# Expert layers of a two-layer encoder step: the last item's down weights go through the gate weights' buffers

## The chip, the cores and the metric

The kernel runs on one core of one Trainium2 chip. The metric is the device time of one execution in microseconds (us); the figure quoted for a kernel is the median of its runs. Engines are named as the profile names them: PE is TensorE, DVE is VectorE, ACT is ScalarE, POOL is GpSimd, SP is SyncE, which here only issues DMAs.

## What is computed

The reference is one inference step of a streaming encoder of two layers (`D_MODEL` 1024) for two groups of rows, 512 prompt frames and 32 sample frames, 544 rows in all. Each layer is a normalised mixer (attention), a gated residual, and then a grouped top-2 mixture of 16 experts with a gated residual. Only the mixture matters here:

```python
def _moe(h, w_router, b_router, w_gate, w_up, w_down):
    ...
    a = jax.nn.silu(jnp.einsum('nd,edf->nef', t, w_gate)) * jnp.einsum('nd,edf->nef', t, w_up)
    a = a * gates[:, :, None].astype(a.dtype)
    return jnp.einsum('nef,efd->nd', a, w_down).reshape(B, T, D)
```

`gates` is zero but for two experts of each row. `w_gate` and `w_up` are 1024 x 512 for each expert, `w_down` is 512 x 1024, all float32.

## The kernel before

**Items.** The router stage sorts the 1088 pairs of a row and an expert by expert and cuts them into items of up to 128 rows with one expert each; 18 items in layer 0 and 16 in layer 1 in the profiled execution. The expert stage `moe0` or `moe1` handles one item after another. For an item, the rows are gathered from DRAM and transposed, multiplied by the gate and by the up weights (8 steps of 128 along the 1024 each), silu(gate) times up gives the activations, these are transposed, and multiplied by the down weights (4 steps along the 512, two halves of 512 output columns). The result, scaled by the row's gate, is scattered to DRAM by an indirect DMA from POOL. After the last item, the stage `combine` reads both results of every row back and adds them to `x`.

**Split products.** float32 is multiplied as three products of rounded parts: high x high, high x low, low x high (`split_product`, lines 580 to 584). So each weight slab is split after it has landed: ACT copies it rounded into a second buffer (the high part, `split_high`, line 1899), then DVE and POOL subtract that from the landed slab in place (the low part; DVE's pieces 0, 2 and 3 in `split_low`, line 1905, POOL's piece 1 at line 2373). A slab of 2 MB is 128 x 4096, in four pieces of 128 x 1024, and comes in two DMAs of two pieces each.

**Buffers.** There is one landed slab and one high slab for each of gate, up and down: `m_low` is the three parts of `ring`, `m_high` lies in `hT`, `work` and `arena` (line 1877). So a load can start only when PE is done with the slab's previous user. In the expert stage SP (`moe_sync`, its loads at line 2128) takes them in this order: in `turn(n)` it waits until the gate product of item n is done and loads the gate weights of item n+1, waits for the up product of n and loads up for n+1, waits for the down product of item n-1 and loads down for item n.

**Order of each engine.** PE does gate(n), transposes of the rows of n+1, up(n), down(n-1), transposes of the activations of n (line 2215). The down product is thus one item behind. In the code, `down_before(n)` is the product of item n-1, and counts of the down slab carry the same shift. After the loop each engine has the last item written out. On PE it is gate(last), up(last), down of the item before the last, transposes, down of the last item, which in this code is `down_before(last + 1)`. On ACT it is: activations high (line 2272), the second half of the up split, silu (line 2268), the split of the down weights of the item before the last, `results_before(last)` (two scaled copies out of the banks, line 2280, which first wait for the scatter of the item before them, `s["y"]`), `act_high_before(last + 1)` (line 2272), the split of the last item's down weights, `results_before(last + 1)`. On DVE: the low part of the activations (line 2339), low splits of up and down, `product(last)` (line 2335), `act_low_before(last + 1)` (line 2339), the low split of the last down weights. On POOL: its piece of the down split, `rows_out_before(last)` (line 1994 copies the row numbers, line 1997 is the scatter), its piece of the last down split, `rows_out_before(last + 1)`. SP waits for `s["d"] >= last`, so for the down product of the item before the last, loads the last item's down weights, waits for all scatters (`s["y"]`), and issues the reads for `combine` (lines 2168 and 2172).

The stages are separated by `phase_end`: PE, ACT, DVE and POOL all have to reach it. SP isn't held by it, but its own order is fixed.

Of the kernel before, what the change touches and what calls it, by code (L numbers as in the profile page):

```python
# [18 lines left out]
ACT = mybir.ActivationFunctionType  # L19
# [56 lines left out]
def encoder_step(nc, a, out, rope_dram):  # L76
    ctx = ExitStack()
    with ctx:
# [3 lines left out]
        def sems(prefix, *names):  # L82
            return {n: ctx.enter_context(nc.semaphore(f"{prefix}_{n}")) for n in names}
# [1768 lines left out]
        def out_pool(pool, l):  # L1852
            s, o = NORM, 2 * l + 1
            for j in OUT_POOL:
# [8 lines left out]

        MO = sems("mo", "wg0", "wg1", "wu0", "wu1", "wd0", "wd1", "hi_g", "hi_u", "hi_d", "lo_g", "lo_u", "lo_d",
                  "lop_g", "lop_u", "lop_d", "x", "tx", "xh", "xl", "g", "sg", "u", "a", "at", "ah", "al", "d", "ev", "y", "now_tok", "now_out")
        m_x = arena[:, 0:1024]
        m_xh = arena[:, 1024:2048].rearrange("p (k c) -> p k c", k=KD)
# [6 lines left out]
        SLAB = KD * CB  # L1876
        m_low = {"g": ring[:, 0, :], "u": ring[:, 1, :], "d": ring[:, 2, :]}
        m_high = {"g": hT_flat[:, 0:SLAB], "u": work[:, 0:SLAB], "d": arena[:, 10240:10240 + SLAB]}

        def piece(v, q):  # L1880
            return v[:, SLAB // 4 * q:SLAB // 4 * (q + 1)]
# [9 lines left out]

            return 0 if l == 0 else eng.value_load(n_items[0:1, 4:5], min_val=9, max_val=MAX_ITEMS)

        def split_high(act, c, n, *pieces):

            for q in pieces:
                if q in (0, 2):
                    act.wait_ge(MO[f"w{c}{q // 2}"], 16 * n if c == "d" else 16 * n + 16)
                act.activation(r32(piece(m_high[c], q)), piece(m_low[c], q), ACT.Copy).then_inc(MO[f"hi_{c}"], 1)  # L1899

        def split_low(dve, c, n, *pieces):

            for q in pieces:
                dve.wait_ge(MO[f"hi_{c}"], 4 * n + q + 1)
                dve.tensor_tensor(r32(piece(m_low[c], q)), piece(m_low[c], q), f32(piece(m_high[c], q)),  # L1905
                                  ALU.subtract).then_inc(MO[f"lo_{c}"], 1)


# [211 lines left out]
        def moe_sync(sp, l):  # L2120
            s = MO
            slabs = {"g": (a["w_gate"][l], KD), "u": (a["w_up"][l], KD), "d": (a["w_down"][l], KE)}

            def load(c, e):
                w, k = slabs[c]
                w = w[bass.ds(e, 1), :, :].rearrange("a (p k) c -> p (a k) c", k=k)
                for h in range(2):
                    sp.dma_start(m_low[c][:, SLAB // 2 * h:SLAB // 2 * (h + 1)].rearrange("p (k c) -> p k c", k=k // 2),
                                 w[:, k // 2 * h:k // 2 * (h + 1), :]).then_inc(s[f"w{c}{h}"], 16)


            sp.wait_ge(OUT["mm"], 10 * (l + 1))
            for c in "gud":
                load(c, 0)
            o = NORM_NO[f"norm_ffn{l}"]
            sp.wait_ge(NORM["shifted"], 3 * o + 3)
            sp.wait_ge(NORM["shift_v"], 2 * o + 2)
            sp.dma_start(moe_in[0:SEQ, :].rearrange("(t p) d -> p t d", p=P), h_rows[:, 0:NT, :]).then_inc(RT["h"], 16)
            sp.dma_start(moe_in[SEQ:TOK, :], h_rows[0:DEC, NT, :]).then_inc(RT["h"], 16)
            sp.wait_ge(g["phase"], PH[f"route{l}"])  # L2140
            first, last, end = first_item(sp, l), item_no(sp, "last"), item_no(sp, "end")

            def expert(n):
                i = nc.s_assert_within(n - first, 0, MAX_ITEMS - 1, skip_runtime_bounds_check_because="n is an item of this layer")
                return sp.value_load(item_expert[0:1, bass.ds(i, 1)], min_val=0, max_val=NE - 1)

            def turn(n, down):

                e = expert(n + 1)
                sp.wait_ge(s["g"], n + 1)  # L2150
                load("g", e)
                sp.wait_ge(s["u"], n + 1)
                load("u", e)
                if down:
                    e = expert(n)
                    sp.wait_ge(s["d"], n)
                    load("d", e)

            turn(first, False)
            with sp.Fori(first + 1, last) as n:  # L2160
                turn(n, True)
            e = expert(last)
            sp.wait_ge(s["d"], last)
            load("d", e)
            sp.wait_ge(s["y"], 16 * end)
            for t in range(TILES):
                if t < NT:
                    sp.dma_start(arena[:, 2 * D * t:2 * D * (t + 1)].rearrange("p (c d) -> p c d", c=2),
                                 moe_out.rearrange("(c n) d -> n c d", c=2)[P * t:P * (t + 1), :, :]).then_inc(CO[f"y{t}"], 32)
                else:  # L2170
                    for c in range(2):
                        sp.dma_start(c_y[t][c][0:DEC, :], moe_out[TOK * c + SEQ:TOK * (c + 1), :]).then_inc(CO[f"y{t}"], 16)

        def moe_pe(pe, l):
# [40 lines left out]
                    last_ = nc.tensor.transpose(bank[6][:, P * k:P * k + P], ak[:, k, :], ident[:, :])  # L2215
                last_.then_inc(s["at"], 1)

            def down_before(n):

                pe.wait_ge(s["al"], n)  # L2220
                hi, lo = (r32(v["d"].rearrange("p (k c) -> p k c", k=KE)) for v in (m_high, m_low))
                for k in range(KE):
                    wait_piece("d", n, k)
                    for h in range(2):
                        c = slice(CB * h, CB * h + CB)
                        last_ = split_product(bank[4 + h][:, :], r32(m_ah[:, k, :]), r32(m_al[:, k, :]), hi[:, k, c],
                                              lo[:, k, c], k == 0, k == KE - 1)
                last_.then_inc(s["d"], 1)
# [13 lines left out]
            gate_or_up("u", last)  # L2242
            down_before(last)
            turn_act(last)
            down_before(last + 1)
            phase_end("pe", pe)

        def moe_act(act, l):
# [57 lines left out]
            split("u", last, 2, 3)  # L2306
            silu(last)
            split("d", last, 0, 1, 2, 3)
            results_before(last, last_1)
            act_high_before(last + 1)  # L2310
            split("d", last + 1, 0, 1, 2, 3)
            results_before(last + 1, last)
            phase_end("act", act)

        def moe_dve(dve, l):
# [44 lines left out]
            split("u", last, 2, 3)  # L2360
            split("d", last, 0, 2, 3)
            product(last)
            act_low_before(last + 1)
            split("d", last + 1, 0, 2, 3)
            phase_end("dve", dve)

        def moe_pool(pool, l):
            first, last = first_item(pool, l), item_no(pool, "last")

            def split(c, n):  # L2370
                pool.wait_ge(MO[f"hi_{c}"], 4 * n + 2)
                settle(pool)
                pool.tensor_tensor(r32(piece(m_low[c], 1)), piece(m_low[c], 1), f32(piece(m_high[c], 1)),  # L2373
                                   ALU.subtract).then_inc(MO[f"lop_{c}"], 1)

            def item(n):
# [26 lines left out]
                turn(n, True)  # L2403
            turn(last_1, False)
            split("d", last)
            rows_out_before(last)
            split("d", last + 1)
            rows_out_before(last + 1)
            phase_end("pool", pool)

# [189 lines left out]
```

## Time and profile before

| | us |
|---|---|
| median of 3 runs | 1777.8 |
| lowest and highest of them | 1762.39, 1778.7 |
| the profiled execution, its time | 1779.54 |
| the profiled execution, its span | 1777.8 |
| its mean granted TensorE clock | 0.913 |

The page's times and all rows below come from the profiled execution, and count from the start of its span. The two expert stages end at about 903 us and 1732 us. "Line" is the line of the kernel; buffer numbers are left out of names, so `ring` is any of the three landed slabs and `arena_r` among other things the high part of down, `hT_r` that of gate, `work_r` that of up.

### The profile page before, as it was taken

To read this page: it belongs to the slowest core of one execution; us is meant where nothing else is said; L and a number is where in the kernel's file an instruction comes from. 1 tells how busy PE (TensorE), PEld (TensorE's weight loads), DVE (VectorE), ACT (ScalarE), POOL (GpSimd) and SP (SyncE) were. 2 spreads that over 40 slices of the span, in tenths; PEclk is the share of its full clock that TensorE was granted. 3 is DMA by queue.
4 is the path that set the end of the run, shared out by engine and by line. 5 is a ranking of instruction groups with operands and counts; after the bars stand their busy time and mean duration, and the time that the engine had idled before them with its cause. 6 is when DMAs were issued, how large, how long until landed. Compare 5 with 4: busy or idle time off the path is not lost. (4 is left out here: it accounts for less than half of the span.)

```text
span 1777.8 us, 22790 instructions
## 1 busy us (share of the span) xinstructions
PE 1496.0 (84%) x7971; PEld 1170.2 (66%) x7979; DVE 1027.2 (58%) x1341; ACT 863.7 (49%) x1512; POOL 498.2 (28%) x383
## 2 busy tenths in 40 slices
PE   3399999997947999999916999999889399999970
PEld 0387777764736877777715877777567277887760
DVE  0545532225455899899856433343363568889865
ACT  2233334445124877777614333343341268878751
POOL 1200111110104666566421000000001246666531
PEclk8699999998977999999956999999889599999985
DMA  8245553133044999899661333442421379999944
GB/s 282 74 159 188 177 183 102 67 127 102 1 192 155 380 350 347 341 360 347 264 239 50 97 102 102 130 145 97 155 71 63 140 287 374 368 368 370 351 188 173
DMA packets 148608, 358.62 MB, mean 202 GB/s; under 512 B 18660, under 2 KB 80868, under 8 KB 122420
## 3 DMA queue, kind: packets, MB, share of 16 engines
q1 hardware_dynamic: 136184, 333.25, 52.0%
q0 software_dynamic: 12352, 24.40, 3.7%
q8 instruction: 45, 0.74, 0.2%
q14 instruction: 27, 0.22, 0.0%
HBM read 341.87 MB, written 33.56 MB: 211 GB/s over the span
## 5 line engine op out<-in xcount | busy, mean ns | idle before, releaser
L583 PE MATMUL bank<-ring_r,arena_r 128*128 128x512 f32 x816 | 323.9, 397 | 0.0
L582 PE MATMUL bank<-ring_r,hT_r 128*128 128x384 f32 x640 | 238.7, 373 | 4.3 <-DVE ring_r L637 4.3
L584 PE MATMUL bank<-ring_r,work_r 128*128 128x384 f32 x640 | 216.9, 339 | 0.0
L583 PE MATMUL bank<-ring_r,hT_r 128*128 128x384 f32 x640 | 216.7, 339 | 0.0
L1905 DVE TENSOR_TENSOR ring_r<-ring,arena_r 128x1024 fp32r<-128x1024 f32 x102 | 169.5, 1698 | 40.3 <-ACT arena_r L1899 40.2
L1905 DVE TENSOR_TENSOR ring_r<-ring,work_r 128x1024 fp32r<-128x1024 f32 x102 | 175.0, 1741 | 28.6 <-ACT work_r L1899 28.5
L583 PEld LDWEIGHTS bank<-ring_r,arena_r 128*128 128x128 f32 x816 | 157.4, 193 | 31.3
L1905 DVE TENSOR_TENSOR ring_r<-ring,hT_r 128x1024 fp32r<-128x1024 f32 x102 | 145.9, 1458 | 25.0 <-ACT hT_r L1899 23.9
L1899 ACT ACTIVATE hT_r<-ring 128x1024 fp32r<-128x1024 f32 x136 | 136.2, 1054 | 37.7 <-DMA ring<-in_w_gate 37.7
L582 PEld LDWEIGHTS bank<-ring_r,hT_r 128*128 128x128 f32 x640 | 121.3, 190 | 45.5 <-issue 43.5
L1899 ACT ACTIVATE arena_r<-ring 128x1024 fp32r<-128x1024 f32 x136 | 134.6, 1051 | 27.4 <-DMA ring<-in_w_down 27.2
L1899 ACT ACTIVATE work_r<-ring 128x1024 fp32r<-128x1024 f32 x136 | 136.6, 1059 | 7.1 <-DMA ring<-in_w_up 7.0
L1858 POOL TENSOR_TENSOR arena<-arena,bc 128x1024 f32<-128x1024 f32 (+1 forms) x6 | 14.3, 2386 | 441.2 <-DVE arena L1844 441.2
L582 PE MATMUL bank<-arena_r 128*128 128x512 f32 x272 | 109.5, 402 | 19.6 <-DVE ring_r L1905 19.6
L583 PEld LDWEIGHTS bank<-ring_r,hT_r 128*128 128x128 f32 x640 | 121.7, 190 | 1.2 <-issue 0.7
L584 PEld LDWEIGHTS bank<-ring_r,work_r 128*128 128x128 f32 x640 | 121.0, 189 | 0.0
L2373 POOL TENSOR_TENSOR ring_r<-ring,arena_r 128x1024 fp32r<-128x1024 f32 x34 | 91.7, 2696 | 95.9 <-ACT arena_r L1899 95.9
L582 PE MATMUL bank<-hT_r,arena_r 128*128 128x512 f32 x272 | 114.5, 421 | 3.1 <-ACT arena_r L2262 3.0
L584 PE MATMUL bank<-hT_r,arena_r 128*128 128x512 f32 x272 | 110.8, 407 | 0.0
L582 PE MATMUL bank<-work_r,arena_r 128*128 128x512 f32 x272 | 109.2, 402 | 0.0
L680 ACT ACTIVATE arena<-bank 128x384 f32<-128x384 f32 (+1 forms) x48 | 23.4, 488 | 175.0 <-PE bank L584 175.0
L584 PE MATMUL bank<-arena_r 128*128 128x512 f32 x272 | 107.9, 397 | 0.0
(357 smaller groups left out, 2980.6 us busy)
## 6 DMA issues: line engine op xcount, KB each, us to landing
ring<-in_w_gate SPq DMA_DIRECT2D x68, 1024.0 KB, 6.9
ring<-in_w_up SPq DMA_DIRECT2D x68, 1024.0 KB, 7.3
ring<-in_w_down SPq DMA_DIRECT2D x68, 1024.0 KB, 7.2
bc<-in_w_ada SPq DMA_DIRECT2D x40, 1024.0 KB, 6.8
bc<-in_w_in_even SPq DMA_DIRECT2D x64, 192.0 KB, 3.9
bc<-in_w_in_odd SPq DMA_DIRECT2D x64, 192.0 KB, 3.5
ring<-in_w_ada SPq DMA_DIRECT2D x4, 2048.0 KB, 11.8
arena<-moe_out SPq DMA_DIRECT2D x8, 1024.0 KB
```

Of the source, the lines that this page charges most:

```text
L582: nc.tensor.matmul(acc, rows_hi, w_hi, start=first, stop=False)
L583: nc.tensor.matmul(acc, rows_hi, w_lo, start=False, stop=False)
L584: return nc.tensor.matmul(acc, rows_lo, w_hi, start=False, stop=last)
L680: act.activation(fu_rows[b % 2][0:rows(t), t, :], bank[n % 2][0:rows(t), 0:BW], ACT.Copy).then_inc(FU["ev_a"], 1)
L1858: pool.tensor_tensor(h_rows[0:r, t, :], h_rows[0:r, t, :], scale_shift(f"norm_ffn{l}", t)[1], ALU.add).then_inc(s["shifted"], 1)
L1899: act.activation(r32(piece(m_high[c], q)), piece(m_low[c], q), ACT.Copy).then_inc(MO[f"hi_{c}"], 1)
L1905: dve.tensor_tensor(r32(piece(m_low[c], q)), piece(m_low[c], q), f32(piece(m_high[c], q)), ALU.subtract).then_inc(MO[f"lo_{c}"], 1)
L2373: pool.tensor_tensor(r32(piece(m_low[c], 1)), piece(m_low[c], 1), f32(piece(m_high[c], 1)), ALU.subtract).then_inc(MO[f"lop_{c}"], 1)
```

## The change

For the last item of each layer alone, the down weights are loaded into the gate slab (`ring` part 0) and their high part is written to `hT`, where the gate's high part lay. SP issues that load when the gate product of the last item is done instead of when the down product of the item before the last is done. The load has two semaphores of its own, `wl0` and `wl1`; those of the down slab are raised by SP after its wait for the scatters so that their counts stay right. On ACT the high split moves ahead of `results_before(last)`; on DVE the low split moves ahead of `act_low_before(last + 1)`; on POOL its piece moves ahead of `rows_out_before(last)`. PE takes its operands from the other buffers. The diff, cut to its core:

```diff
+        def slab_of(c, last_down):
+            return "g" if last_down else c
...
-        def split_high(act, c, n, *pieces):
+        def split_high(act, c, n, *pieces, last_down=None):
+            v = slab_of(c, last_down is not None)
             for q in pieces:
                 if q in (0, 2):
-                    act.wait_ge(MO[f"w{c}{q // 2}"], 16 * n if c == "d" else 16 * n + 16)
-                act.activation(r32(piece(m_high[c], q)), piece(m_low[c], q), ACT.Copy).then_inc(MO[f"hi_{c}"], 1)
+                    if last_down is not None:
+                        act.wait_ge(MO[f"wl{q // 2}"], 16 * last_down + 16)
+                    else:
+                        act.wait_ge(MO[f"w{c}{q // 2}"], 16 * n if c == "d" else 16 * n + 16)
+                act.activation(r32(piece(m_high[v], q)), piece(m_low[v], q), ACT.Copy).then_inc(MO[f"hi_{c}"], 1)
...
             e = expert(last)
-            sp.wait_ge(s["d"], last)
-            load("d", e)
+            sp.wait_ge(s["g"], last + 1)
+            load("d", e, last_down=True)
             sp.wait_ge(s["y"], 16 * end)
+            for h in range(2):
+                sp.sem_inc(s[f"wd{h}"], 16)
...
             down_before(last)
             turn_act(last)
-            down_before(last + 1)
+            down_before(last + 1, last_down=True)
             phase_end("pe", pe)
...
             split("d", last, 0, 1, 2, 3)
+            split_high(act, "d", last + 1, 0, 1, 2, 3, last_down=l)
             results_before(last, last_1)
             act_high_before(last + 1)
-            split("d", last + 1, 0, 1, 2, 3)
             results_before(last + 1, last)
...
             split("d", last, 0, 2, 3)
             product(last)
+            split_low(dve, "d", last + 1, 0, 2, 3, last_down=True)
             act_low_before(last + 1)
-            split("d", last + 1, 0, 2, 3)
             phase_end("dve", dve)
...
             split("d", last)
+            split("d", last + 1, last_down=True)
             rows_out_before(last)
-            split("d", last + 1)
             rows_out_before(last + 1)
             phase_end("pool", pool)
```

## Rows read from the trace of the kernel before

**Rows 1.** The page: an engine's busy time, share of the span, instructions.

```profile
PE 1496.0 (84%) x7971; PEld 1170.2 (66%) x7979; DVE 1027.2 (58%) x1341; ACT 863.7 (49%) x1512; POOL 498.2 (28%) x383
```

**Rows 2.** Timeline of PE, end of layer 1: start us, duration us, engine, line.

```profile
1710.20 0.47 PE L582 MATMUL bank<-arena_r 128*128 128x512 f32 x1 [1.27 <-DVE ring_r L1905]
...
1715.76 0.63 PE L2215 MATMUL bank<-ident,arena 128*128 128x128 f32 x4
1723.29 0.79 PE L582 MATMUL bank<-arena_r 128*128 128x512 f32 x1 [6.89 <-DVE ring_r L1905]
```

**Rows 3.** Timeline of ACT, end of layer 1.

```profile
1703.44 0.60 ACT L2268 ACTIVATE arena<-bank 128x512 f32<-128x512 f32 x1 [0.23 <-PE bank L584]
1703.94 3.89 ACT L1899 ACTIVATE arena_r<-ring 128x1024 fp32r<-128x1024 f32 x4
1716.22 1.27 ACT L2280 ACTIVATE arena<-bank,slot_gate 128x512 f32<-128x512 f32 x2 [8.39 <-PE bank L584]
...
1720.92 2.00 ACT L1899 ACTIVATE arena_r<-ring 128x1024 fp32r<-128x1024 f32 x2 [2.94 <-DMA ring<-in_w_down]
1723.82 2.00 ACT L1899 ACTIVATE arena_r<-ring 128x1024 fp32r<-128x1024 f32 x2 [0.90 <-DMA ring<-in_w_down]
1732.04 1.27 ACT L2280 ACTIVATE arena<-bank,slot_gate 128x512 f32<-128x512 f32 x2 [6.22 <-PE bank L584]
```

**Rows 4.** Timeline of DVE, end of layer 1.

```profile
1706.63 5.70 DVE L1905 TENSOR_TENSOR ring_r<-ring,arena_r 128x1024 fp32r<-128x1024 f32 x3
1712.24 0.68 DVE L2335 TENSOR_TENSOR arena<-bank,arena 128x512 f32<-128x512 f32 x1
1718.01 0.69 DVE L2339 TENSOR_TENSOR arena_r<-bank,arena_r 128x512 fp32r<-128x512 f32 x1 [5.09 <-ACT arena_r L2272]
1722.01 1.23 DVE L1905 TENSOR_TENSOR ring_r<-ring,arena_r 128x1024 fp32r<-128x1024 f32 x1 [3.30 <-ACT arena_r L1899]
```

**Rows 5.** Timeline of POOL, end of layer 1.

```profile
1693.10 3.28 POOL L2373 TENSOR_TENSOR ring_r<-ring,hT_r 128x1024 fp32r<-128x1024 f32 x1 [2.36 <-ACT hT_r L1899]
...
1706.12 2.85 POOL L2373 TENSOR_TENSOR ring_r<-ring,arena_r 128x1024 fp32r<-128x1024 f32 x1 [1.64 <-ACT arena_r L1899]
...
1734.52 1.00 POOL L1997 DMA_INDIRECT moe_out<-arena,now_out  x1 [0.86 <-POOL now_out L1994]
```

**Rows 6.** Timeline of SP: its DMA issues, two answers.

```profile
1716.11 0.85 SPq L2128 DMA_DIRECT2D ring<-in_w_down  x2
...
1737.79 2.09 SPq L2168 DMA_DIRECT2D arena<-moe_out  x4
```

**Rows 7.** Windows: stretch, busy PE PEld DVE ACT POOL, PEclk, DMA share, GB/s.

```profile
1704.50:1706.00 1.50, 1.50 (x8) 1.24 (x7) 1.50 (x2) 1.50 (x3) 0.00 (x0) 1.00 0.39 156
...
1723.29:1731.90 8.61, 8.60 (x24) 6.49 (x24) 2.80 (x2) 2.00 (x2) 2.20 (x1) 0.64 0.08 30
```

**Rows 8.** Instructions of one tile: its DMAs' landing, for ring, then for moe_out.

```profile
DMA to landing us min/median/max: 4.8/7.1/17.9
...
DMA to landing us min/median/max: 3.2/7.1/12.7
```

**Rows 9.** Timelines of PE, DVE and ACT, end of layer 0.

```profile
894.49 0.79 PE L582 MATMUL bank<-arena_r 128*128 128x512 f32 x1 [6.94 <-DVE ring_r L1905]
...
889.09 0.69 DVE L2339 TENSOR_TENSOR arena_r<-bank,arena_r 128x512 fp32r<-128x512 f32 x1 [4.98 <-ACT arena_r L2272]
...
902.94 1.26 ACT L2280 ACTIVATE arena<-bank,slot_gate 128x512 f32<-128x512 f32 x2 [4.69 <-PE bank L584]
```

**Rows 10.** Shorter stalls of PE in the item loops, and windows behind them.

```profile
810.29 0.72 PE L2215 MATMUL bank<-ident,arena 128*128 128x128 f32 x4 [1.73 <-DVE arena L2335]
...
1435.47 0.84 PE L2215 MATMUL bank<-ident,arena 128*128 128x128 f32 x4 [3.30 <-DVE arena L2335]
...
811.00:814.80 3.80, 3.80 (x11) 3.01 (x11) 3.80 (x5) 3.30 (x4) 2.89 (x3) 0.55 0.99 374
655.60:659.00 3.40, 3.40 (x15) 2.80 (x16) 3.40 (x5) 3.26 (x4) 2.49 (x3) 1.00 0.99 419
```

More of the change, by code:

```diff
@@ L1859, in out_pool @@
             phase_end("pool", pool)
-        MO = sems("mo", "wg0", "wg1", "wu0", "wu1", "wd0", "wd1", "hi_g", "hi_u", "hi_d", "lo_g", "lo_u", "lo_d",
+        MO = sems("mo", "wg0", "wg1", "wu0", "wu1", "wd0", "wd1", "wl0", "wl1", "hi_g", "hi_u", "hi_d", "lo_g", "lo_u", "lo_d",
                   "lop_g", "lop_u", "lop_d", "x", "tx", "xh", "xl", "g", "sg", "u", "a", "at", "ah", "al", "d", "ev", "y", "now_tok", "now_out")
@@ L1892, in layer_first, with split_low @@
             return 0 if l == 0 else eng.value_load(n_items[0:1, 4:5], min_val=9, max_val=MAX_ITEMS)
-        def split_high(act, c, n, *pieces):
+        def split_high(act, c, n, *pieces, last_down=None):
+            v = slab_of(c, last_down is not None)
             for q in pieces:
                 if q in (0, 2):
-                    act.wait_ge(MO[f"w{c}{q // 2}"], 16 * n if c == "d" else 16 * n + 16)
-                act.activation(r32(piece(m_high[c], q)), piece(m_low[c], q), ACT.Copy).then_inc(MO[f"hi_{c}"], 1)
-        def split_low(dve, c, n, *pieces):
+                    if last_down is not None:
[3 more added lines that the diff above has]
+                act.activation(r32(piece(m_high[v], q)), piece(m_low[v], q), ACT.Copy).then_inc(MO[f"hi_{c}"], 1)
+        def split_low(dve, c, n, *pieces, last_down=False):
+            v = slab_of(c, last_down)
             for q in pieces:
                 dve.wait_ge(MO[f"hi_{c}"], 4 * n + q + 1)
-                dve.tensor_tensor(r32(piece(m_low[c], q)), piece(m_low[c], q), f32(piece(m_high[c], q)),
+                dve.tensor_tensor(r32(piece(m_low[v], q)), piece(m_low[v], q), f32(piece(m_high[v], q)),
                                   ALU.subtract).then_inc(MO[f"lo_{c}"], 1)
@@ L2122, in moe_sync, with load @@
             slabs = {"g": (a["w_gate"][l], KD), "u": (a["w_up"][l], KD), "d": (a["w_down"][l], KE)}
-            def load(c, e):
+            def load(c, e, last_down=False):
                 w, k = slabs[c]
@@ L2127, in load @@
                 for h in range(2):
-                    sp.dma_start(m_low[c][:, SLAB // 2 * h:SLAB // 2 * (h + 1)].rearrange("p (k c) -> p k c", k=k // 2),
-                                 w[:, k // 2 * h:k // 2 * (h + 1), :]).then_inc(s[f"w{c}{h}"], 16)
+                    sp.dma_start(m_low[slab_of(c, last_down)][:, SLAB // 2 * h:SLAB // 2 * (h + 1)].rearrange("p (k c) -> p k c", k=k // 2),
+                                 w[:, k // 2 * h:k // 2 * (h + 1), :]).then_inc(s[f"wl{h}" if last_down else f"w{c}{h}"], 16)
             sp.wait_ge(OUT["mm"], 10 * (l + 1))
@@ L2216, in turn_act, with down_before @@
                 last_.then_inc(s["at"], 1)
-            def down_before(n):
+            def down_before(n, last_down=False):
                 pe.wait_ge(s["al"], n)
-                hi, lo = (r32(v["d"].rearrange("p (k c) -> p k c", k=KE)) for v in (m_high, m_low))
+                hi, lo = (r32(v[slab_of("d", last_down)].rearrange("p (k c) -> p k c", k=KE)) for v in (m_high, m_low))
                 for k in range(KE):
@@ L2368, in moe_pool, with split @@
             first, last = first_item(pool, l), item_no(pool, "last")
-            def split(c, n):
+            def split(c, n, last_down=False):
+                v = slab_of(c, last_down)
                 pool.wait_ge(MO[f"hi_{c}"], 4 * n + 2)
                 settle(pool)
-                pool.tensor_tensor(r32(piece(m_low[c], 1)), piece(m_low[c], 1), f32(piece(m_high[c], 1)),
+                pool.tensor_tensor(r32(piece(m_low[v], 1)), piece(m_low[v], 1), f32(piece(m_high[v], 1)),
                                    ALU.subtract).then_inc(MO[f"lop_{c}"], 1)
```

## The prediction

> **What bounds the kernel now.** I read the page first: PE is busy 84% of the span, far above any other engine [rows 1], so in the item loops the matmuls set the time, and an edit outside PE's path is worth what it takes out of PE's stalls or out of a stage's end. The change touches only the end of each expert stage, so I went to the timelines there, PE first and then, for each thing PE waits for, the engine that releases it. The reader is to see one long stall. PE ends the transposes of the last activations at 1715.76 + 0.63 = 1716.39 and starts the last down product at 1723.29, after 6.89 us of nothing, released by a DVE low split [rows 2]. Layer 0 has the same stall, 6.94 us [rows 9]. Everything behind it is a chain with no other work in it: down product, ACT's copies, scatter, SP's reads, combine. So a microsecond less here is a microsecond less in the span, once in each layer.
>
> What fills the stall: the down slab is free only when the down product before is done, so SP issues the load at 1716.11 [rows 6]. ACT gets the halves at 1720.92 and 1723.82, that is 4.8 and 7.7 us after the issue [rows 3]. DVE's first piece runs from 1722.01 for 1.23 us, and PE starts 0.05 us behind it [rows 2, 4]. The stall costs a second time: the granted clock over the product is 0.64 [rows 7]. From PE's start to ACT's first copy it takes 1732.04 - 1723.29 = 8.75 us; the product before it, the same 24 matmuls, took 1716.22 - 1710.20 = 6.02 us [rows 2, 3]. In layer 0 it is 902.94 - 894.49 = 8.45 us [rows 9].
>
> **The change, part by part.** I work out layer 1 and carry it to layer 0.
>
> *The load.* Silu starts at 1703.44, when the last gate product is done [rows 3], so SP issues at about 1703.6 in place of 1716.11. SP has nothing else to issue between; the next thing in its queue is the wait for the scatters, which is later in any case. The gate slab and its high part in `hT` have no later reader in the stage. The DMA engines are still 39% busy at 1704.5 to 1706.0 with the load before and not at all after that [rows 7], so the load meets at most its tail. With the 4.8 and 7.7 us from above the halves are there at about 1708.4 and 1711.3. The longest landing of any load into the ring is 17.9 us [rows 8], which is the bound on the bad side.
>
> *ACT.* It ends the split before at 1703.94 + 3.89 = 1707.83 and is idle for 8.39 us until 1716.22 [rows 3]. The four copies (2.00 us for two) go into that hole: 1708.4 to 1710.4 and 1711.3 to 1713.3. Behind them in ACT's queue are the copies of the results and the activations' high part, due at 1716.22: 2.9 us of slack. Cost nothing; were the cover gone, ACT would hand all its delay to PE.
>
> *DVE and POOL.* Here is a cost. DVE's three pieces took 5.70 us from 1706.63, though one takes 1.23 us alone; POOL's piece ran until 1706.12 + 2.85 = 1708.97 [rows 4, 5], and 5.70 less three pieces of 1.14 us (one behind the other they overlap a little) is 2.3 us, the time from 1706.63 to POOL's end. So DVE stood still while POOL ran. The other way round, POOL's piece at 1693.10 took 3.28 us [rows 5]. After the first piece, at about 1710.1, there is now this to do in turn: two pieces of the slab before (2.3 us), POOL's new piece, ready when ACT's second copy is at about 1710.5 (2.3 us), and three new DVE pieces (3.4 us). That ends at 1718.1. `product`, 0.68 us and reading a bank, either runs beside POOL's piece or stands in the row: 1718.8. `act_low_before` could not start before 1718.01 in any case [rows 4], waiting for ACT. So it ends between 1718.8 and 1719.5 where it ended at 1718.70, and PE starts between 1718.85 and 1719.55. I take the middle, 1719.2: the rows show both orders of the two engines, and not who is next when both wait. `product` itself may come 2.3 us later, ending at 1715.2; PE needs it at 1715.76 [rows 2], so it is just hidden, as is DVE's third piece to within 0.4 us. Start of the last down product: 1723.29 - 1719.2 = 4.1 us earlier (3.7 to 4.4). In layer 0 the activations' low part ends at 889.09 + 0.69 = 889.78 [rows 9]; with the same 0.5 us behind it PE starts at 890.3 instead of 894.49, 4.2 us earlier.
>
> The Trainium skill says of this pair of engines (SBUF — State Buffer, section "SBUF: two separate sides") that a DVE operation with two SBUF inputs and a GpSimd one hold a shared port pair exclusively for the whole instruction and the other blocks. The trace agrees, with the 5.70 us. Without that rule the DVE chain would end at about 1716, the activations' low part at the old 1718.70, and each layer would gain 0.5 us more.
>
> *The clock.* The stall shrinks from 6.9 to 1719.2 - 1716.4 = 2.8 us. No stall of that size ends in a product in the loops, so I bound it from both sides. Ten stalls in the item loops end at the transposes of the activations. Eight last 1.69 to 1.74 us; after six of them the clock stayed whole and after two it was low for a while, one shown of each [rows 10]. Two last 3.3 to 3.4 us, and both were followed by a low clock. In the window behind such a fall the grant is 0.55 over 3.80 us [rows 10], so 3.8 x 0.45 = 1.7 us of full-speed work is lost. A stall of 2.8 us is nearer to 3.3 than to 1.7, so I take it that the clock falls, and costs 1.7 us: 6.0 + 1.7 = 7.7 us in place of 8.75 and 8.45, a gain of 1.0 and 0.7. The bounds are nothing gained (the full 2.7 us lost as now) and 2.7 and 2.4 gained (clock held).
>
> *The scatter.* ACT's last copies wait for the scatter before, which POOL issues behind its piece. POOL is done by 1713.5 at the latest and the scatter is due at about 1718.8, as now. Scatters land after 3.2 us at best, 7.1 in the middle, 12.7 at worst [rows 8]. The final one, with no load beside it, took 1737.79 - 1734.52 = 3.3 us to SP's next issue [rows 5, 6]. After the change this one has no load beside it either: landed at about 1722, and ACT wants it at 1719.2 + 7.7 = 1726.9. Hidden.
>
> *Two increments on SP* stand between the scatters' landing and the reads for combine. No row shows one there; next to an issue of 0.43 us (two in 0.85, rows 6) I put both at 0.05 us a layer, with 0 and 0.4 as bounds [rows 6].
>
> Sum: 4.1 + 4.2 + 1.0 + 0.7 - 0.1 = 9.9 us. The profiled execution took 1779.54 us by its own time, which gives 1769.6. It lies 1.7 us above the median of the runs, so I take the sum from the median: 1777.8 - 9.9 = 1767.9, said as 1768 us.
>
> **The rivals.** *The clock is held in both layers.* For it: six of eight stalls of 1.7 us. Against it: both of 3.3 us. The gain is then 8.3 + 2.7 + 2.4 - 0.1 = 13.3 us, 1764.5 us. If it falls for as long as now, the gain is 8.2 us, 1769.6 us; both are in the range.
>
> *The scatter takes the place of the load.* If it lands as late as the worst, 12.7 us after 1718.8, ACT starts its copies at 1731.5 instead of 1726.9. That takes 4.6 us of each layer's 5: 1777 us. Against it, that the DMA engines would be empty then.
>
> *The early load arrives no sooner, or is hidden anyway.* If the end of the stage hung on something else, nothing would move: 1778 us. Against it: PE's releaser is the low split of that slab in both layers.
>
> *Slower: ACT stands in front of its own results.* Its four copies now come ahead of the results and of the activations' high part. With the second half landed at L, ACT is done with the copies at L + 2.0, the results take 1.2, the high part 0.6, DVE's low part 0.7, so PE starts at L + 4.5. That is later than 1723.29 once L is beyond 1718.8, 15.2 us after the issue. At the ring's longest landing, 17.9 us, L is 1721.5, PE starts at 1726.0, 2.7 us later than now in each layer: 1783 us. Against it: the middle landing is 7.1 us even in the loops with the queue full [rows 8], and here it is empty.
>
> **How the numbers follow.** Chances: the forecast 0.50, clock held in one or both layers 0.30, scatter 0.07, no effect 0.07, slower 0.06. The three runs before spread over 16 us, with one 15 us below the others; if the changed kernel's median falls among its low runs it is near 1753. So the range is 1752 to 1776: above it the last two cases and some of the scatter's. About 1% is what a measurement of this kernel can tell from no change, that is 17.8 us. No sum here reaches it; only the spread of the runs does, in about a fifth of the cases, mostly with the clock held. Faster by over 1%: 0.19; within 1%: 0.78; slower: 0.03, half of the slower case, since its own price is under 1%.
>
> **What would show it.** Right: a w_down issue by SP within 0.3 us of the last silu, ACT's last four L1899 copies (now `hT_r<-ring`) before the results, and a PE stall of 2.5 to 3.2 us before the last down product, released by L2339 and no longer by L1905. DVE's last splits end beside 1718 to 1719. The stage's last down product takes 6.0 to 8.7 us to ACT's copy. Wrong: a stall under 2.4 us (no cost of DVE and POOL against each other), the last L2280 released by the scatter, a grant of 1.00 over the last product in both layers, or a difference between the two kernels that lies before 1703 us of layer 1 or in the stretch from 906 to 1416 us.

## The result, and the profile after

| | before | changed |
|---|---|---|
| median of 20 runs, us | 1771.8 | 1759.7 |
| lowest and highest, us | 1762.39, 1783.65 | 1748.23, 1767.21 |
| profiled execution, span, us | 1777.8 | 1763.3 |

The ratio of the two is 0.9934, with a 95% interval of 0.9914 to 0.9953: 11.7 us less (8.3 to 15.2) of the 1771.8; the two medians themselves lie 12.1 us apart. With 20 runs of each the kernel before sits at 1771.8 us, not at the 1777.8 of its first three.

Lines in the changed kernel are 8 to 12 higher: L1899 is now L1907 (ACT's high copies), L1905 is L1914 (DVE's low pieces), L2373 is L2385 (POOL's), L2215 is L2226 (transposes), L2268 is L2279 (silu), L2272 is L2283 (the activations' high part), L2280 is L2291 (results), L2335 is L2346 (the product silu times up), L2339 is L2350 (the activations' low part). In the kernels of the experiments some of them move by another 3 to 6: L2286 and L2353 below are the activations' high and low part, L2294 the results.

PE's timeline at the end of the two expert stages, layer 0 first, which answers to [rows 2, 9]:

```profile
885.45 0.79 PE L582 MATMUL bank<-hT_r,arena_r 128*128 128x512 f32 x1 [3.94 <-DVE arena_r L2350]
...
1706.53 0.63 PE L2226 MATMUL bank<-ident,arena 128*128 128x128 f32 x4
1710.07 0.79 PE L582 MATMUL bank<-hT_r,arena_r 128*128 128x512 f32 x1 [2.90 <-DVE arena_r L2350]
```

The last down product now reads `hT_r`, its stall is 3.94 and 2.90 us instead of 6.94 and 6.89, and it ends with DVE's low part of the activations (L2350), no longer with a low split of weights. ACT's timeline, first the two marks of layer 0 that are used below, then layer 1, answering to [rows 3]:

```profile
870.15 0.60 ACT L2279 ACTIVATE arena<-bank 128x512 f32<-128x512 f32 x1 [0.62 <-PE bank L584]
...
893.85 1.27 ACT L2291 ACTIVATE arena<-bank,slot_gate 128x512 f32<-128x512 f32 x2 [10.54 <-PE bank L584]
...
1694.49 0.60 ACT L2279 ACTIVATE arena<-bank 128x512 f32<-128x512 f32 x1 [0.42 <-PE bank L584]
...
1697.21 2.01 ACT L1907 ACTIVATE arena_r<-ring 128x1024 fp32r<-128x1024 f32 x2 [0.22 <-DMA ring<-in_w_down]
1701.84 2.01 ACT L1907 ACTIVATE hT_r<-ring 128x1024 fp32r<-128x1024 f32 x2 [2.62 <-DMA ring<-in_w_down]
1704.38 2.01 ACT L1907 ACTIVATE hT_r<-ring 128x1024 fp32r<-128x1024 f32 x2 [0.53 <-DMA ring<-in_w_down]
1706.99 1.27 ACT L2291 ACTIVATE arena<-bank,slot_gate 128x512 f32<-128x512 f32 x2 [0.61 <-PE bank L584]
1708.15 0.60 ACT L2283 ACTIVATE arena_r<-bank 128x512 fp32r<-128x512 f32 x1
1717.56 1.27 ACT L2291 ACTIVATE arena<-bank,slot_gate 128x512 f32<-128x512 f32 x2 [8.81 <-PE bank L584]
```

ACT's four copies lie in the hole before the results. The waits in brackets at 1701.84 and 1704.38 are for the new load, that at 1697.21 for the load before it. DVE in layer 1, then in layer 0, then POOL's two rows, answering to [rows 4, 5]:

```profile
1697.43 5.70 DVE L1914 TENSOR_TENSOR ring_r<-ring,arena_r 128x1024 fp32r<-128x1024 f32 x3
1703.05 0.68 DVE L2346 TENSOR_TENSOR arena<-bank,arena 128x512 f32<-128x512 f32 x1
1703.65 1.21 DVE L1914 TENSOR_TENSOR ring_r<-ring,hT_r 128x1024 fp32r<-128x1024 f32 x1
1705.47 3.87 DVE L1914 TENSOR_TENSOR ring_r<-ring,hT_r 128x1024 fp32r<-128x1024 f32 x2 [0.61 <-ACT hT_r L1907]
1709.26 0.68 DVE L2350 TENSOR_TENSOR arena_r<-bank,arena_r 128x512 fp32r<-128x512 f32 x1
...
879.16 5.56 DVE L1914 TENSOR_TENSOR ring_r<-ring,hT_r 128x1024 fp32r<-128x1024 f32 x3
884.64 0.68 DVE L2350 TENSOR_TENSOR arena_r<-bank,arena_r 128x512 fp32r<-128x512 f32 x1
...
878.95 2.41 POOL L2385 TENSOR_TENSOR ring_r<-ring,hT_r 128x1024 fp32r<-128x1024 f32 x1 [2.53 <-ACT hT_r L1907]
...
1704.03 3.10 POOL L2385 TENSOR_TENSOR ring_r<-ring,hT_r 128x1024 fp32r<-128x1024 f32 x1 [4.26 <-ACT hT_r L1907]
```

"Port" below is the access to SBUF that DVE and POOL hold by turns (the prediction, part on DVE and POOL). In layer 0 POOL has it from 878.95 to 881.36, and DVE's three pieces take 5.56 us and end at 884.72; the activations' low part follows at once, with no wait in brackets. SP's timeline, the loads and then the first reads for `combine`, answering to [rows 6]:

```profile
1687.48 8.01 SPq L2137 DMA_DIRECT2D ring<-in_w_down  x4
1723.42 2.19 SPq L2179 DMA_DIRECT2D arena<-moe_out  x4
```

And the windows over the two last products, with the granted clock ahead of the last two columns, answering to [rows 7]:

```profile
885.45:893.85 8.40, 8.27 (x24) 6.31 (x24) 0.00 (x0) 0.00 (x1) 0.14 (x1) 0.68 0.11 42
1710.07:1717.56 7.49, 7.34 (x24) 5.61 (x24) 0.00 (x0) 0.00 (x0) 1.00 (x1) 0.77 0.10 40
```

**Where the 14.5 us between the two profiled spans went.** I cut each span at two marks that both traces show: the start of the last item's silu and the start of ACT's last pair of result copies. Call the stretch between them T.

| stretch | before | changed | difference |
|---|---|---|---|
| start to the last silu of layer 0 | 874.67 | 870.15 | -4.5 |
| T, layer 0 | 28.27 | 23.70 | -4.6 |
| to the last silu of layer 1 | 800.50 | 800.64 | +0.1 |
| T, layer 1 | 28.60 | 23.07 | -5.5 |
| to the end | 45.76 | 45.74 | 0.0 |

So 10.1 us come from the two stretches that the change touches. The 4.5 us ahead of them are not its work: the code there is the same. Over the ten profiled executions of this study (two of them of the changed kernel) the last silu of layer 0 starts anywhere from 865 to 881 us, whatever the kernel. That spread of 16 us is nearly that of the whole time (19 to 21 us over the 20 runs of each kernel), so T is the better measure of an edit here, and whole times need many runs. T has a spread of its own: in the four layers of the two profiles of the changed kernel it is 21.3 to 23.9 us, nearly all of it in the time of the last product.

### The profile page after: what moved, and what is told of

The parts are those of the page before. It is cut to its first block and busy times, and to the rows that moved or that the text cites. A ratio compares the mean times of both kernels' runs of the same rounds, so it can differ in the third digit from the quotient of the medians.

```text
span 1763.3 us, 22802 instructions
## 1 busy us (share of the span) xinstructions
PE 1489.4 (84%) x7979; PEld 1166.0 (66%) x7979; DVE 1012.9 (57%) x1341; ACT 865.1 (49%) x1512; POOL 502.0 (28%) x383
## 5 line engine op out<-in xcount | busy, mean ns | idle before, releaser
L1914 DVE TENSOR_TENSOR ring_r<-ring,work_r 128x1024 fp32r<-128x1024 f32 x102 | 171.5, 1707 | 35.1 <-ACT work_r L1907 35.1
L1914 DVE TENSOR_TENSOR ring_r<-ring,arena_r 128x1024 fp32r<-128x1024 f32 x96 | 158.4, 1686 | 29.3 <-ACT arena_r L1907 29.2
L1907 ACT ACTIVATE hT_r<-ring 128x1024 fp32r<-128x1024 f32 x144 | 144.3, 1054 | 48.3 <-DMA ring<-in_w_gate 43.5
L1914 DVE TENSOR_TENSOR ring_r<-ring,hT_r 128x1024 fp32r<-128x1024 f32 x108 | 144.5, 1366 | 29.0 <-ACT hT_r L1907 28.0
L1907 ACT ACTIVATE arena_r<-ring 128x1024 fp32r<-128x1024 f32 x128 | 127.8, 1052 | 34.5 <-DMA ring<-in_w_down 34.2
L1907 ACT ACTIVATE work_r<-ring 128x1024 fp32r<-128x1024 f32 x136 | 136.6, 1058 | 14.9 <-DMA ring<-in_w_up 14.9
L1858 POOL TENSOR_TENSOR arena<-arena,bc 128x1024 f32<-128x1024 f32 (+1 forms) x6 | 14.3, 2385 | 438.7 <-DVE arena L1844 438.7
L582 PE MATMUL bank<-hT_r,arena_r 128*128 128x512 f32 x288 | 122.3, 425 | 10.0 <-DVE arena_r L2350 6.8
L584 PE MATMUL bank<-hT_r,arena_r 128*128 128x512 f32 x288 | 118.1, 410 | 0.0
L2385 POOL TENSOR_TENSOR ring_r<-ring,arena_r 128x1024 fp32r<-128x1024 f32 x32 | 88.6, 2768 | 83.7 <-ACT arena_r L1907 83.7
L2385 POOL TENSOR_TENSOR ring_r<-ring,hT_r 128x1024 fp32r<-128x1024 f32 x36 | 91.4, 2540 | 62.8 <-ACT hT_r L1907 49.5
L582 PE MATMUL bank<-work_r,arena_r 128*128 128x512 f32 x272 | 109.2, 402 | 0.0
L584 PE MATMUL bank<-work_r,arena_r 128*128 128x512 f32 x272 | 106.4, 391 | 0.0
## 6 DMA issues: line engine op xcount, KB each, us to landing
ring<-in_w_ada SPq DMA_DIRECT2D x4, 2048.0 KB, 12.1
```

Source lines behind the costliest of these rows:

```text
L582: nc.tensor.matmul(acc, rows_hi, w_hi, start=first, stop=False)
L584: return nc.tensor.matmul(acc, rows_lo, w_hi, start=False, stop=last)
L1858: pool.tensor_tensor(h_rows[0:r, t, :], h_rows[0:r, t, :], scale_shift(f"norm_ffn{l}", t)[1], ALU.add).then_inc(s["shifted"], 1)
L1907: act.activation(r32(piece(m_high[v], q)), piece(m_low[v], q), ACT.Copy).then_inc(MO[f"hi_{c}"], 1)
L1914: dve.tensor_tensor(r32(piece(m_low[v], q)), piece(m_low[v], q), f32(piece(m_high[v], q)), ALU.subtract).then_inc(MO[f"lo_{c}"], 1)
L2385: pool.tensor_tensor(r32(piece(m_low[v], 1)), piece(m_low[v], 1), f32(piece(m_high[v], 1)), ALU.subtract).then_inc(MO[f"lop_{c}"], 1)
```

## The experiments

T is cut once more below: S from the silu to PE's start of the last down product, and the product from there to ACT's copies. All from one profiled execution for each kernel, in us, layer 0 / layer 1. S of the changed kernel lies between 15.2 and 15.6 in its four layers, so S shows a difference of half a microsecond, where T shows it only if the products agree. The ratios are of whole times, with runs of the kernel before taken beside them.

| kernel | stall of PE before the product | S | product | T | ratio to before (95%) |
|---|---|---|---|---|---|
| before | 6.9 / 6.9 | 19.8 / 19.9 | 8.45 / 8.75 | 28.3 / 28.6 | 1 |
| changed | 3.9 / 2.9 | 15.3 / 15.6 | 8.40 / 7.49 | 23.7 / 23.1 | 0.9934 (0.9914 to 0.9953) |
| changed, again | 2.9 / 4.2 | 15.4 / 15.2 | 5.88 / 8.69 | 21.3 / 23.9 | 0.9947 (0.9914 to 0.9979) |
| late load | 12.2 / 12.1 | 24.8 / 25.0 | 8.77 / 8.02 | 33.6 / 33.0 | 1.0056 (1.0022 to 1.0091) |
| old order | 3.8 / 3.8 | 16.3 / 15.2 | 8.54 / 7.34 | 24.8 / 22.5 | 0.9995 (0.9961 to 1.0028) |
| DVE does all | 2.7 / 2.4 | 15.2 / 15.4 | 7.38 / 7.40 | 22.6 / 22.8 | 0.9935 (0.9902 to 0.9967) |
| 12 fillers | none | 15.2 / 15.4 | 5.89 / 5.93 | 21.1 / 21.3 | 0.9909 (0.9880 to 0.9938) |
| swap | 2.9 / 2.8 | 15.4 / 15.3 | 8.68 / 7.51 | 24.1 / 22.8 | 0.9916 (0.9884 to 0.9948) |
| swap, DVE does all | 1.8 / 1.8 | 14.9 / 14.3 | 7.50 / 5.91 | 22.4 / 20.2 | 0.9944 (0.9913 to 0.9975) |
| the same, 6 fillers | 0.4 / 0.4 | 14.3 / 14.3 | 5.90 / 5.91 | 20.2 / 20.2 | 0.9911 (0.9873 to 0.9950) |

**The load late, the rest as changed.**

```diff
-            sp.wait_ge(s["g"], last + 1)
+            sp.wait_ge(s["d"], last)
             load("d", e, last_down=True)
```

> The changed kernel with one line put back: SP waits for the down product of the item before the last ahead of the last down load, as before; buffers and the new order on ACT, DVE and POOL stay. T is the time from the start of the last item's silu to the start of the last pair of scaled result copies: before 28.3 and 28.6 us (layers 0 and 1), changed 23.7 and 23.1. Theory (the early issue is the gain, and the new order alone is a loss because ACT's copies stand ahead of the results and of the activations' high part): ACT's four copies end some 9.7 us after the issue, PE starts 4.5 us after the second half has landed, T is 33 to 34 us in both layers, the kernel about 10 us slower than before and 20 slower than the changed one. Rival (only the release of the slab counts, the order doesn't): T as before, 28 to 29 us, and the time of the kernel before.

Measured: T 33.55 and 33.02 us, the kernel 0.56% slower than before, 9.9 us of 1771. The timeline of layer 1, ACT's rows and then PE's:

```profile
1702.63 3.90 ACT L1907 ACTIVATE arena_r<-ring 128x1024 fp32r<-128x1024 f32 x4
1719.66 2.00 ACT L1907 ACTIVATE hT_r<-ring 128x1024 fp32r<-128x1024 f32 x2 [13.14 <-DMA ring<-in_w_down]
1722.10 2.00 ACT L1907 ACTIVATE hT_r<-ring 128x1024 fp32r<-128x1024 f32 x2 [0.43 <-DMA ring<-in_w_down]
1724.01 1.25 ACT L2291 ACTIVATE arena<-bank,slot_gate 128x512 f32<-128x512 f32 x2
1725.15 0.59 ACT L2283 ACTIVATE arena_r<-bank 128x512 fp32r<-128x512 f32 x1
1735.16 1.26 ACT L2291 ACTIVATE arena<-bank,slot_gate 128x512 f32<-128x512 f32 x2 [9.42 <-PE bank L584]
...
1727.14 0.79 PE L582 MATMUL bank<-hT_r,arena_r 128*128 128x512 f32 x1 [12.06 <-DVE arena_r L2350]
```

ACT waits 13.14 us for the load with the results of an item whose product is done standing behind that wait, then needs 4.4 us of copies, 1.1 us of results and the high part. This is the slower rival of the prediction, brought about. Issued at 1714.8 the second half was there at 1722.10, PE started 5.0 us later; the rival's 4.5 us was near. With the late load the new order is a loss, S being 5 us longer than before, and the early issue is what the change lives on.

**The load early, the old order.**

```diff
-            split_high(act, "d", last + 1, 0, 1, 2, 3, last_down=l)
             results_before(last, last_1)
             act_high_before(last + 1)
+            split_high(act, "d", last + 1, 0, 1, 2, 3, last_down=l)
```

with the same move on DVE and POOL.

> The changed kernel with the early load kept and the splits of the last down weights put back behind the results and the activations on ACT, DVE and POOL. Theory (the new order is worth the copies that otherwise run after the results): ACT's first copy starts 1.8 us after its results do, PE's stall is about 4.0 us instead of 2.9 and 3.9, the low clock lasts as long as in the kernel before or nearly, T is 24.6 to 25.6 us in both layers, 1 to 2.5 us a layer more than with the change. Rival (the early load alone is the gain): T as with the change, 23.1 and 23.7 us.

Measured: T 24.83 and 22.54 us, stalls of 3.76 and 3.83 us, released by a low split again. The timeline of layer 1, rows of PE, ACT, DVE and POOL:

```profile
1705.63 0.80 PE L582 MATMUL bank<-hT_r,arena_r 128*128 128x512 f32 x1 [3.83 <-DVE ring_r L1914]
...
1701.62 1.26 ACT L2291 ACTIVATE arena<-bank,slot_gate 128x512 f32<-128x512 f32 x2 [4.64 <-PE bank L584]
1702.77 0.60 ACT L2283 ACTIVATE arena_r<-bank 128x512 fp32r<-128x512 f32 x1
1703.25 3.90 ACT L1907 ACTIVATE hT_r<-ring 128x1024 fp32r<-128x1024 f32 x4
...
1693.24 1.21 DVE L1914 TENSOR_TENSOR ring_r<-ring,arena_r 128x1024 fp32r<-128x1024 f32 x1
...
1694.05 2.69 POOL L2385 TENSOR_TENSOR ring_r<-ring,arena_r 128x1024 fp32r<-128x1024 f32 x1 [2.96 <-ACT arena_r L1907]
```

Layer 0 is within the expectation (24.6 to 25.6), layer 1 isn't. There ACT's results start 11.2 us after the silu where it was 12.8 us before: DVE's first piece of the item before came ahead of POOL's (1693.24 and 1694.05), so PE's earlier product did not have to wait behind the port as it had at 1710.20 [rows 2]. The mean T is 23.7 us, and 23.0 us over the four layers of the changed kernel; the 0.7 us between them are less than the 1 to 2.5 us expected and inside the spread of T. S says more when layers with the same end of PE's transposes are compared. Where they end 12.5 to 12.7 us after the silu, S is 16.3 with the old order (layer 0) and 15.4 and 15.6 with the new one. Where they end after 11.0 to 11.4 us, S is 15.2 with the old order (layer 1) and 15.2 and 15.3 with the new one. So the new order gave 0.7 to 0.9 us where the earlier product ended late and nothing where it ended early, in one layer of the old order for each. The whole times differ by more: this kernel's interval (0.9961 to 1.0028) lies above that of the first set of runs of the changed kernel (0.9914 to 0.9953), though it overlaps that of the second (0.9914 to 0.9979). One profiled execution doesn't show where the rest would lie, and it stays open.

**DVE does POOL's piece.** PE waits for it on a semaphore of its own, `lol`.

```diff
+            dve.wait_ge(s["hi_d"], 4 * (last + 1) + 2)
+            dve.tensor_tensor(r32(piece(m_low["g"], 1)), piece(m_low["g"], 1), f32(piece(m_high["g"], 1)),
+                              ALU.subtract).then_inc(s["lol"], 1)
...
-            split("d", last + 1, last_down=True)
```

> The changed kernel with POOL's piece of the last down weights given to DVE (four DVE pieces, POOL idle there; one semaphore more). Theory (DVE stands still while POOL's piece runs, 2.3 us, which costs more than a fourth piece of 1.1 us): PE's stall goes from 3.9 to about 3.0 us in layer 0 and from 2.9 to about 2.4 in layer 1, released by DVE's low part of the activations right behind ACT's high part; T 0.5 to 0.9 us less a layer, more where the shorter stall spares low clock. Rival (DVE is bound by its own number of pieces): the stall grows by 1.1 us in layer 0 and by up to 0.6 in layer 1.

Measured: the stalls are 2.66 and 2.44 us, but that is PE ending later. S is 15.2 and 15.4, against a mean of 15.4 with the change; 0.1 us gained, not 0.5 to 0.9. DVE's timeline in layer 1:

```profile
1704.54 2.35 DVE L1914 TENSOR_TENSOR ring_r<-ring,hT_r 128x1024 fp32r<-128x1024 f32 x2
1707.43 0.69 DVE L2353 TENSOR_TENSOR arena_r<-bank,arena_r 128x512 fp32r<-128x512 f32 x1 [0.55 <-ACT arena_r L2286]
```

DVE is done at 1706.89, 0.55 us ahead, and then waits for ACT's high part of the activations. So both readings were half right: with POOL's piece the port holds DVE up, but its end is only just later than ACT's, which takes its place at once.

**Twelve filling matmuls in the stall.** They multiply what lies in the buffers of the rows and of the up weights' high part into bank 2, and nobody reads the result.

```diff
             turn_act(last)
+            hi_u = r32(m_high["u"].rearrange("p (k c) -> p k c", k=KD))
+            for i in range(12):
+                nc.tensor.matmul(bank[2][:, :], r32(m_xh[:, i % KD, :]), hi_u[:, i % KD, :], start=i == 0, stop=i == 12 - 1)
             down_before(last + 1, last_down=True)
```

> The changed kernel with 12 extra matmuls of 128 x 512 on PE in the stall before the last down product of each layer, into a bank that nobody reads; their results are used nowhere. They take 12 x 0.23 = 2.8 us. Theory (the low clock over the last product comes from the stall): the clock stays whole, the product takes 6.0 us to ACT's copy in place of 8.4 and 7.5 us, T is about 21.4 to 21.6 us in both layers, the kernel 3 to 4 us faster than with the change. Rival (the clock falls for another reason, or the fillers hold the product up): the product takes 7.5 to 8.4 us as now, or starts later by what the fillers take beyond the stall.

Measured: PE's timeline at the end of layer 0.

```profile
893.21 3.00 PE L2258 MATMUL bank<-work_r,arena_r 128*128 128x512 f32 x12
896.14 0.49 PE L582 MATMUL bank<-hT_r,arena_r 128*128 128x512 f32 x1
```

The window over the last product there:

```profile
896.00:902.00 6.00, 5.90 (x25) 4.42 (x24) 0.01 (x1) 0.00 (x0) 1.00 (x1) 1.00 0.15 59
```

The fillers end as the product becomes ready, S is unchanged (15.2 and 15.4), and the product takes 5.89 and 5.93 us at a whole clock. T is 21.12 and 21.32, as expected or just under, 1.8 us a layer below the changed kernel's mean of 23.0. With PE busy up to the product its clock was whole in both layers, so the stall is a condition of the low clock over it; the next run shows that it is not the only one. By the whole times the gain isn't shown: 0.9909 (0.9880 to 0.9938) overlaps both intervals of the changed kernel.

**The changed kernel again, and three more, on one chip.**

> The changed kernel itself, beside the next three on the same chip. All theories: 0.993 of the time before, T 23 to 24 us in both layers, and the last product begun behind a stall of 2.9 to 3.9 us with a low clock.

Measured: 0.9947 as expected, S of 15.4 and 15.2 as in the first profile, and T 23.9 in layer 1; but layer 0 missed, with a product of 5.88 us and T 21.3, and the stall of layer 1 was 4.2 us. PE's timeline in the second profile of the changed kernel, layers 0 and 1:

```profile
880.39 0.49 PE L582 MATMUL bank<-hT_r,arena_r 128*128 128x512 f32 x1 [2.91 <-DVE arena_r L2350]
...
1695.91 0.79 PE L582 MATMUL bank<-hT_r,arena_r 128*128 128x512 f32 x1 [4.23 <-DVE arena_r L2350]
```

Its windows over the two products:

```profile
880.39:886.27 5.88, 5.76 (x24) 4.41 (x24) 0.00 (x0) 0.00 (x0) 1.00 (x1) 1.00 0.15 61
1695.91:1704.60 8.69, 8.54 (x24) 6.47 (x24) 0.00 (x0) 0.00 (x0) 0.14 (x1) 0.65 0.09 34
```

Behind a stall of 2.91 us the clock was whole, behind one of 2.90 us in the first profile it was 0.77 over the product. The same kernel and the same stall give both, which a sum from one trace can't see.

**Swap: the last product in banks 0 and 1, ACT makes the high part first.**

```diff
-                        last_ = split_product(bank[4 + h][:, :], r32(m_ah[:, k, :]), r32(m_al[:, k, :]), hi[:, k, c],
+                        last_ = split_product(bank[(0 if last_down else 4) + h][:, :], r32(m_ah[:, k, :]), r32(m_al[:, k, :]), hi[:, k, c],
...
-            results_before(last, last_1)
             act_high_before(last + 1)
-            results_before(last + 1, last)
+            results_before(last, last_1)
+            results_before(last + 1, last, 0)
```

> The changed kernel with the last down product written into banks 0 and 1 instead of 4 and 5, so that ACT can make the activations' high part ahead of the scaled copies of the item before. Theory (once the load is early, DVE with POOL's piece in its way ends last in the stall, not ACT): the stall is released by the activations' low part, which starts right behind DVE's last piece and not behind ACT; PE starts 15.0 to 15.4 us after the silu as with the change, T within 0.5 us of it. Rival (ACT's order is the bound): the 1.2 us of the copies come out of the stall in both layers.

Measured, the timeline of layer 1, a row of ACT and two of DVE:

```profile
1704.00 0.60 ACT L2283 ACTIVATE arena_r<-bank 128x512 fp32r<-128x512 f32 x1 [1.34 <-PE bank L2226]
...
1700.45 5.53 DVE L1914 TENSOR_TENSOR ring_r<-ring,hT_r 128x1024 fp32r<-128x1024 f32 x3
1705.90 0.68 DVE L2350 TENSOR_TENSOR arena_r<-bank,arena_r 128x512 fp32r<-128x512 f32 x1
```

ACT's part is ready at 1704.60, DVE's pieces end at 1705.98, and PE's stall is released by what DVE does next. S is 15.4 and 15.3, as with the change and as expected.

**Swap and DVE does all; then with six fillers.**

> Both together: banks 0 and 1 with the new ACT order, and DVE doing POOL's piece of the last down weights. Theory: with DVE free early the 1.2 us of ACT's copies now count; the stall is 1.6 to 1.8 us in both layers, T 1 us less than with DVE's fourth piece alone, and the clock holds in some layers. Rival: T as with DVE's fourth piece alone, 22.6 to 22.8 us.

> The same with 6 extra matmuls of 128 x 512 (1.4 us, into a bank nobody reads) in what is left of the stall. Theory: the clock is whole over the last product, which takes 6.0 us to ACT's copy; T 19.8 to 20.5 us in both layers, 6 to 7 us less than with the change over both, the fastest of all kernels here. Rival (the clock needs no help at a stall of 1.7 us, or the fillers stand in the way): T as without them.

PE's timeline at the product's start in each layer of the first of the two:

```profile
894.14 0.50 PE L582 MATMUL bank<-hT_r,arena_r 128*128 128x512 f32 x1 [1.80 <-DVE arena_r L2353]
...
1712.91 0.49 PE L582 MATMUL bank<-hT_r,arena_r 128*128 128x512 f32 x1 [1.81 <-DVE arena_r L2353]
```

Its windows over the products, with two stretches of the first:

```profile
894.14:895.20 1.06, 1.05 (x5) 0.88 (x6) 0.00 (x0) 0.00 (x1) 0.19 (x1) 1.00 0.00 0
895.50:898.80 3.30, 3.30 (x10) 2.52 (x9) 0.00 (x0) 0.00 (x0) 0.85 (x1) 0.50 0.29 113
894.14:901.64 7.50, 7.37 (x24) 5.55 (x24) 0.00 (x0) 0.00 (x1) 1.19 (x2) 0.77 0.13 51
1712.91:1718.82 5.91, 5.76 (x24) 4.41 (x24) 0.00 (x0) 0.00 (x0) 1.18 (x2) 1.00 0.13 51
```

Each edit alone gave 0.0 to 0.1 us of S, both together 0.5 and 1.0 us (14.9 and 14.3, after 15.4 on the mean of the changed kernel). In layer 0 PE ended the transposes 13.1 us after the silu and in layer 1 after 12.5, and that is the difference between the two layers. Two engines end within about half a microsecond of each other, and only relieving both moves PE. T is 22.4 and 20.2, where 1 us less than the 22.6 and 22.8 of DVE's fourth piece alone was expected. The stalls of 1.80 and 1.81 us are again one with a fall and one without, 7.50 and 5.91 us of product. The window over layer 0's product with six fillers:

```profile
883.40:889.20 5.80, 5.69 (x24) 4.33 (x24) 0.00 (x0) 0.00 (x0) 1.18 (x2) 1.00 0.16 63
```

With them both products take 5.9 us, S is 14.3 and T 20.2 in both layers, 2.8 us a layer under the changed kernel's mean of 23.0, so 5.5 us over both where 6 to 7 were expected. That is the shortest T of all and beats both kernels by the trace. By the whole times it can't be told from twelve fillers alone (0.9911 and 0.9909): what is left between these kernels, 2 to 6 us, is inside intervals some 10 to 14 us wide. Swap with DVE's fourth piece even reads 0.9944, with T 3.3 us under the changed kernel's mean over both layers. Its profiled execution has the second latest silu of layer 0, at 879.25, but one execution doesn't explain the median of ten. So the gains of the last three kernels over the changed one are read from T and S of their traces, and no whole time shows them.

## Why the prediction was right, and which of its terms were off

The forecast was 1768 us, from a gain of 9.9 us; the runs give 11.7 us (8.3 to 15.2) and the two touched stretches of the profile 10.1. It lies within 1% of no change and is clear of it, as the sum said. The time itself came out 8 us below the forecast mainly because the median of the kernel before, which the sum was taken from, is 1771.8 over 20 runs and not 1777.8.

The mechanism held. That 9.9 and 10.1 lie so close is in part luck: S gained 8.8 us where 8.3 were forecast, the products 1.3 where 1.7 were, and the second profile of the same kernel gives 11.7 us over the two stretches, because one of its products ran at a whole clock. One of the prediction's signs of being wrong came true by its words, a difference ahead of the last items: the 4.5 us before the silu of layer 0. As shown above it is within the spread of that mark, so it tells nothing of the change.

- *The stall is the term, once in each layer.* Right. S fell by 4.5 and 4.3 us (forecast 4.2 and 4.1), and putting the issue back lost it and more.
- *The load arrives 4.8 and 7.7 us after its issue.* Mis-sized. SP's last issue lies at the end of its merged row, 1695.49 - 0.85 = 1694.64 (two issues take 0.85 us [rows 6]), 0.15 us after the silu, and ACT got the halves at 1701.84 and 1704.38, 7.2 and 9.7 us later. I had taken the landing of a load that had none before it, though [rows 7] showed the load before still on its way; it hadn't landed when ACT wanted its second half (a wait of 0.22 us at 1697.21 in the changed kernel's trace). The 2.9 us of slack that I gave to ACT were 0.6 us in layer 1, and in layer 0 ACT's results follow its copies with no wait. Layer 0 of the kernel before, whose rows I had not worked out, already had its second half 9.0 us after the issue (887.24 to 896.24). What the error cost isn't shown. The activations' low part follows DVE's last piece and not ACT, which was 0.6 us earlier; but DVE itself had waited 0.61 us for ACT's third copy (the row at 1705.47), and that copy for the load. By these rows my estimate is at most about 0.6 us in layer 1.
- *DVE and POOL in turn.* Right in size and by another way. The DVE chain was forecast to end 14.7 to 15.4 us after the silu, and it ended after 14.85 us in layer 1 and 14.57 in layer 0. PE's start was forecast at 15.8 and 15.6 and came at 15.6 and 15.3. The order was another: in layer 1 DVE did its three old pieces, `product` and its new piece 0 before POOL's new piece. The two experiments with DVE's fourth piece show that it is one of two bounds that end nearly together, the other being ACT's order. In layer 0 three pieces take 5.56 us beside POOL's 2.41, and with POOL idle two take 2.35 us. The Trainium skill (SBUF — State Buffer, section "SBUF: two separate sides") has one of the two engines block the other for a whole instruction; the trace agrees, 5.56 being 2.0 us more than three times the half of 2.35, and POOL's piece lies beside them for 2.2 us.
- *The stall would be 2.8 us.* Right in layer 1, 2.90. In layer 0 it was 3.94, since PE had ended the transposes earlier, 11.4 us after the silu and not 12.9; that is outside the 2.5 to 3.2 us that the prediction gave as its sign. It moves the stall and not the start.
- *The clock falls and costs 1.7 us.* Right in kind; its size is a spread. In four layers of the changed kernel the product took 8.40, 7.49, 5.88 and 8.69 us, a mean of 7.6 beside the forecast of 7.7, from 5.9 to 8.7; a single value inside such a spread is right by luck. The rival with the clock held came true in one of four.
- *The scatter is hidden.* Right: ACT's last results are released by PE in both layers.
- *The two increments on SP*, 0.05 us a layer. Somewhat small: in layer 1 from ACT's last results to SP's first read it took 5.75 us [rows 3, 6] and now 1723.42 - 1717.56 = 5.86.
- *The slower rival* (ACT in front of its own results) needed the second half 15.2 us after the issue; it came after 9.7. With the load late (the first experiment) it cost 5 us a layer.

## What to carry to other kernels

A load can be given the buffer that is freed first when it is the last user of the stage; that pays only if the engines that prepare the data are free in the time gained, and an in-order engine that takes the preparation ahead of its results must be sure that the load is early. For the landing of a load moved into a busy queue take the rows of the busy queue. When an edit alone gives nothing, look for a second engine that ends at nearly the same time, and where PE stalls for two to three microseconds ahead of a product that is on the path, try a few matmuls on data at hand: here they kept the clock whole over it in four layers of four and did not delay it. Without them it was whole in some layers too, and the gain was too small for the whole times to show.

## What the runs showed of the hardware that I had not expected

The granted clock after a short stall isn't a function of the stall's length alone. Stalls of 2.9 us were followed by a product of 5.88 us at a clock of 1.00 in one execution and of 7.49 us at 0.77 in another, stalls of 1.8 us by 5.91 and 7.50 us in two layers of one execution. Nor does the fall need to lie in the stall: the product of 7.50 us began with a granted clock of 1.00 (894.14 to 895.20) and then ran at 0.50, the lower level (895.50 to 898.80), so the clock fell after PE had started again. Filling the stall gave 5.9 us each time, in four of four layers. The Trainium skill (TensorE: Matmul & The Clock Gate, section "HAM oscillation — how this bites in real kernels") has bursts of matmuls start cold after waits for data and advises to keep PE free of long idle gaps. The products behind the longer stalls here agree (0.68 behind 3.94 us, 0.65 behind 4.23 us). The waits of the page's kernel are longer than 1.8 and 2.9 us, and after stalls as short as these the traces show both outcomes.
